# Late queries by early keys of a gated recurrence: two 128x128 products in unused PSUM columns in place of four of 64x64

## The chip, the cores and the metric

The kernel is one program on one core of a Trainium2 chip. The metric is the time of one execution on the device, in microseconds (us). Lower is better. TensorE (PE in the rows, and PEld for its weight loads), VectorE (DVE), ScalarE (ACT), GpSimd (POOL) and the DMA queue of SyncE (SP) run side by side and meet at semaphores.

## The reference, cut to what matters

The network has two layers: an HGRN2 gated linear recurrence (mixer A) and a latent attention (mixer B), for 1024 prompt positions and 8 running streams of 16 positions. Only mixer A's prompt part is touched:

```python
def gla_chunked(q, k, v, log_f, s0, chunk):       # chunk = 64, 8 heads of 128
    b = jnp.cumsum(log_f, axis=2)
    b_mid = b[:, :, mid:mid + 1]
    q_in = q * jnp.exp(b - b_mid)
    k_in = k * jnp.exp(b_mid - b)
    scores = jnp.einsum('bnlhk,bnshk->bnhls', q_in, k_in)
    scores = jnp.where(causal, scores, 0.0)
    o_intra = jnp.einsum('bnhls,bnshv->bnlhv', scores, v)
    ...
    o_inter = jnp.einsum('bnlhk,bnhkv->bnlhv', q * jnp.exp(b), s_prev)
    o = (o_intra + o_inter)
```

## The kernel before, in words

The 1024 prompt positions are 16 chunks of 64. The kernel takes them two at a time, as 8 blocks of 128. Within a block a score tile has 128 keys (partitions) by 128 queries (columns) and four quadrants of 64x64: the early chunk on itself, the late chunk on itself, late queries by early keys, and early queries by late keys, which is empty. The two diagonal quadrants come from one product of `kin` by `qin` and need a causal mask. The quadrant of late queries by early keys needs other decays, so it comes from `k_early` (the block's first 64 positions) by `q_late` (its last 64), and nothing in it is masked. Both operands hold the 8 blocks side by side, 64 columns each.

Phase A runs over 8 heads. `heads` calls `body` nine times: body h projects head h (three projections, `c` = 0, 1, 2: forget gate, query, output gate) and does the recurrence of head h-1 (`gla`) in between. A projection is 3 groups of 384 columns (`tg`) times 8 contraction tiles times 3 products of 384 columns (lines 124, 125, 126: each float32 operand is split into a high and a low part). Its three groups fill columns 0 to 383 of three PSUM banks, `pj[:, i, tg, 0:TG]`; columns 384 to 511 of these banks are not used. The other two banks, `gb`, belong to the recurrence, whose fifteen steps alternate between them.

The recurrence's TensorE work is cut into the steps of `GLA_STEPS`, put between the projection's products at fixed hooks, one hook after each 12 products. The order is written out by hand:

```python
GLA_STEPS = ["K0", "C0", "S0", "SI", "O0", "K1", "C1", "S1", "O1", "OT0", "SO", "SS0", "OT1", "SS1", "SOT"]
STEPS_AT = {3: (0, 1), 5: (2, 3), 7: (4, 5), 9: (6, 7), 11: (8, 9), 13: (10, 11), 15: (12, 13), 17: (14,)}
```

Half 0 has blocks 0 to 3, half 1 blocks 4 to 7. Of each half: K turns keys (line 510), C makes the scores (lines 539 and 544), S makes the chunk states (line 550), O makes the output from the masked scores and from the states (lines 559 and 561), OT turns the output back. Hook 3 is K0 and C0, hook 5 is S0 and SI, hook 7 is O0 and K1, hook 9 is C1 and S1, hook 11 is O1 and OT0. Hooks 3 and 9 lie behind the second of the three groups of projections 0 and 1. TensorE works strictly in this order. A step begins when what was in its bank has been read (`step_out`) and its operands are there. O1 waits for the scores of C1 (`out_of["C1"]`) and for the last state of half 1 (`state_step`).

VectorE has its own order, in `body`. Around half 1 it is: `square(0)`, `keys(1)`, the scan of the gates (line 1064), `normed(0)` (line 1002), `scores(1)` (line 964), four subtractions on the scanned gates (lines 1075 and 1077), `states(1)` (line 984, four in a chain). `scores(n)` is one predicated copy of 128x512 from PSUM to `sct`: mask 1 lets a score through, elsewhere the zeros of the start remain. In the last body (h = 8) there is no projection; the products of the output projection (128x512) stand between the steps, and `states(1)` comes directly behind `scores(1)`.

ScalarE reads a finished projection from its banks: line 773 that of `c` = 0, line 799 that of `c` = 1.

Of the kernel before, what the change touches and what calls it, by code (L numbers as in the profile page):

```python
# [13 lines left out]
P = 128  # L14
# [6 lines left out]
TG = 384  # L21
NTG = T // TG
CH = 64
# [8 lines left out]
BANK = 512  # L32
# [3 lines left out]
def flat(ap):  # L36
    return ap.rearrange("p a b -> p (a b)")
# [190 lines left out]
def phase_mixer_a(nc, k):  # L228
# [17 lines left out]
    q_late = third.take("a_q_late", [NPB, CH])  # L246
    k_early = third.take("a_k_early", [NPB, CH])
    mask_p = third.take("a_mask_p", [4 * P], I32)
# [99 lines left out]
    def buffer_of(odd, c):  # L348

        return (odd * NC + c) % 2  # L350
# [157 lines left out]
    def _(pe):  # L508
# [3 lines left out]
        def blk(x, b):  # L512
            return x[:, b * P:(b + 1) * P]

        def step(i, h):

            s = GLA_STEPS[i]
            bank = i % 2
            if i >= 2:
                step_out(pe, GLA_STEPS[i - 2], h)  # L520
            elif not (isinstance(h, int) and h == 1):

                last = len(GLA_STEPS) - 1
                pe.wait_ge(out_of[GLA_STEPS[last - (last - i) % 2]], h - 1)

            def out(slot, n=1):
                return gb[:, bank, slot * P:(slot + n) * P]

            if s in ("K0", "K1"):
                pe.wait_ge(ident_loaded, 16)  # L530
                pe.wait_ge(operand[0], h)
                for j in range(4):
                    mm = tr(bank, j, blk(kdec, 4 * int(s[1]) + j))
            elif s in ("C0", "C1"):
                pe.wait_ge(operand[1], h)
                pe.wait_ge(operand[2], h)
                for j in range(4):
                    b = 4 * int(s[1]) + j
                    nc.tensor.matmul(out(j), blk(kin, b), blk(qin, b), start=True, stop=True)  # L539
                pe.wait_ge(operand[0], h)  # L540
                pe.wait_ge(operand[3], h)
                for j in range(4):
                    b = 4 * int(s[1]) + j
                    mm = nc.tensor.matmul(gb[0:CH, bank, j * P + CH:(j + 1) * P], k_early[:, b], q_late[:, b], start=True, stop=True)
            elif s in ("S0", "S1"):
                n = int(s[1])
                pe.wait_ge(vn_loaded, h * 16)
                pe.wait_ge(out_of[f"K{n}"], h)
                for j in range(4):
                    mm = nc.tensor.matmul(out(j), kdn[:, j], vn[:, 4 * n + j], start=True, stop=True)  # L550
            elif s in ("O0", "O1"):
                n = int(s[1])
                pe.wait_ge(out_of[f"C{n}"], h)

                step_out(pe, f"S{n}", h)
                pe.wait_ge(operand[3], h)
                for j in range(4):
                    b = 4 * n + j
                    mm = nc.tensor.matmul(out(j), sct[:, j], vn[:, b], start=True, stop=b == 0)  # L559
                    if b:  # L560
                        mm = nc.tensor.matmul(out(j), blk(qex, b), st[:, b], start=False, stop=True)  # L561
            elif s in ("OT0", "OT1", "SOT"):
                n = ["OT0", "OT1", "SOT"].index(s)
                pe.wait_ge(on_ready, h * 3 + (n - 2))
                for j in range(4 if n < 2 else 1):
                    mm = tr(bank, j, on[:, j])
            elif s == "SI":
                tr(bank, 1, blk(kdec, NPB))
                mm = nc.tensor.matmul(out(2), blk(kin, NPB), blk(qin, NPB), start=True, stop=True)
            elif s == "SO":  # L570
                pe.wait_ge(out_of["SI"], h)
                pe.wait_ge(spread_done, h * 2)
                pe.wait_ge(states_loaded, h * 16)
                nc.tensor.matmul(out(0), sct8[:], vn[:, NPB], start=True, stop=False)
                for i in range(NSEQ):
                    mm = nc.tensor.matmul(out(0), qdiag[:, i], sts[:, i], start=False, stop=i == NSEQ - 1)  # L576
            else:
                n = int(s[2])
                mm = nc.tensor.matmul(out(0, 4), kd8[:], flat(vexp[:, 4 * n:4 * n + 4]), start=True, stop=True)  # L579
            mm.then_inc(pe_did[s], 1)  # L580
# [45 lines left out]
        def body(h, odd, proj, gla):  # L626
            if not proj:
                y = [k.bank[:, 4:6], k.bank[:, 0:2], k.bank[:, 2:4]]
                for i in range(-1, len(GLA_STEPS)):
                    if i >= 0:  # L630
                        step(i, h)
                    for row, t in BESIDE_STEPS.get(i, []):
                        pe.wait_ge(row_low, row + 1)
                        pe.wait_ge(o_low, parts_for(row, t))
                        if row == 0:
                            if t != 1:
                                pe.wait_ge(g_out, AH)
                            if t != 0:
                                pe.wait_ge(q_out, AH)
                        rows_product(nc, y[t], sh, row, t)  # L640
                return
            hook = 0
            for c in range(NC):
                i = buffer_of(odd, c)
                pe.wait_ge(wl_ready, h * NC + c + 1)

                if c == 2:
                    pe.wait_ge(z_out, h + 1)
                elif gla:
                    pe.wait_ge((q_out, g_out)[c], h)  # L650
                else:
                    pe.wait_ge(v_out, (len(V_UNITS) - 3, len(V_UNITS))[c])
                for tg in range(NTG):
                    for kt in range(KD):
                        cols = slice(tg * TG, (tg + 1) * TG)
                        mm = product(nc, pj[:, i, tg, 0:TG],
                                     (w_h[i][:, kt], w_l[i][:, kt]),
                                     (k.act_h[:, kt, cols], k.act_l[:, kt, cols]),
                                     kt == 0, kt == KD - 1)
                        if kt == KD - 1 and tg == NTG - 1:  # L660
                            mm.then_inc(proj_done, 1)
                        if kt % 4 == 3:
                            if gla:
                                for n in STEPS_AT.get(hook, ()):
                                    step(n, h)
                            hook += 1

        pe.wait_ge(zeroed, 1)
# [9 lines left out]
    def _(act):  # L678
# [78 lines left out]
        def body(h, odd, proj, gla):  # L757
# [9 lines left out]
            if proj:  # L767
                act.wait_ge(proj_done, h * NC + 1)
                if gla:

                    act.wait_ge(gates[2], h)
                for dst, sign in ((fz, 1.0), (nz, -1.0)):
                    last = nc.scalar.activation(dst[:].rearrange("p (a b) -> p a b", a=3), pj[:, buffer_of(odd, 0), :, 0:TG], ACT.Sigmoid, scale=sign)
                last.then_inc(z_out, 1)
                high(h, odd, 2)

                act.wait_ge(z_out, h + 1)
                if isinstance(h, int):
                    a, b = oml[:, h:h + 1], lb[:, h:h + 1]
                else:  # L780
                    a, b = oml[:, bass.ds(h, 1)], lb[:, bass.ds(h, 1)]
                if isinstance(h, int) and h == 0:
                    act.wait_ge(prep, 7)
                nc.scalar.activation(fz[:], fz[:], ACT.Ln, scale=a, bias=b).then_inc(logf_done, 1)
# [5 lines left out]
            if proj:  # L790
                act.wait_ge(proj_done, h * NC + 2)
                if gla:

                    act.wait_ge(operand[2], h)
                    act.wait_ge(operand[3], h)
                else:
                    for i in range(2):
                        act.wait_ge(v_stored[i], 16 * NT)
                nc.scalar.copy(qq[:].rearrange("p (a b) -> p a b", a=3), pj[:, buffer_of(odd, 1), :, 0:TG]).then_inc(q_out, 1)
                if not (isinstance(h, int) and h == AH - 1):  # L800
                    high(h + 1, 1 - odd, 0)
                else:
                    high_row(0)
                    high_o(0)
# [95 lines left out]
    def _(dve):  # L900
# [52 lines left out]
        def body(h, odd, proj, gla):  # L953
            def bank(s):
                return gb[:, GLA_STEPS.index(s) % 2]
# [5 lines left out]
            def scores(n):  # L961
                dve.wait_ge(zeroed, 5)
                dve.wait_ge(pe_did[f"C{n}"], h)
                nc.vector.copy_predicated(flat(sct[:]), mask_p[:], bank(f"C{n}")).then_inc(out_of[f"C{n}"], 1)

            def states(n):

# [2549 lines left out]
```

## Time and profile before

| | |
|---|---|
| median of three runs | 1863.83 us (1863.42 to 1863.83) |
| the profiled execution, whole | 1863.33 us |
| its span in the trace | 1861.5 us |
| TensorE busy | 1849.0 us, 99% of the span |
| VectorE busy | 1046.2 us, 56% |
| mean granted TensorE clock | 0.998 of full speed |

Times in the timeline are from the span's start. A row of a timeline gives the start, the time from the first start to the last end of the merged instructions, and their count. Matmuls are pipelined: the next one starts before the end of the one before, so what one costs is read from start to start. A float32 matmul of `gb` leaves two records (two passes). The recurrence of heads 1 to 7 (in bodies with a projection) lies between about 150 and 505 us, that of the last body between 505 and 550 us.

### The profile page before, as it was taken

The numbers are of one execution on the slowest core, as the hardware profiler recorded it, in microseconds if no ns is written. First come the engines' busy times: TensorE is split into PE (matmuls) and PEld (weight loads), VectorE is DVE, ScalarE is ACT, GpSimd is POOL, SyncE is SP. The second block draws the span as 40 slices with busy tenths as digits, with TensorE's granted clock in tenths as the row PEclk, the third lists the DMA queues.
The fourth block names the chain that finished last, engine by engine and source line by source line (L and its number), as shares of the span: only waits on it lengthen the run. The fifth ranks groups of instructions, "written<-read, shape, count | busy, mean of one in ns | idle before, by whom it ended". The sixth has DMA issues, their size and how long they took to land.

```text
span 1861.5 us, 30229 instructions
## 1 busy us (share of the span) xinstructions
PE 1849.0 (99%) x11250; PEld 1734.6 (93%) x11250; DVE 1046.2 (56%) x1852; ACT 741.8 (40%) x1307; POOL 429.6 (23%) x341
## 2 busy tenths in 40 slices
PE   9999999999999999999999999999999999999998
PEld 8899999999988999999999999999999999998886
DVE  3126565556768512432466676666766679853642
ACT  4234324333422221221355565555555567651100
POOL 0013133223311010000042432434324344400000
PEclk9999999999999999999999999999999999999999
DMA  8120222222255312233302111111121185553521
GB/s 264 57 87 33 76 83 84 72 83 73 70 195 164 131 46 73 83 100 120 100 27 67 42 55 55 56 51 46 51 75 38 30 255 185 189 203 127 166 86 45
DMA packets 162059, 178.91 MB, mean 96 GB/s; under 512 B 23376, under 2 KB 137424, under 8 KB 161712
## 3 DMA queue, kind: packets, MB, share of 16 engines
q1 hardware_dynamic: 155632, 158.08, 26.8%
q10 hardware_dynamic: 6160, 19.14, 2.9%
q8 instruction: 63, 1.03, 0.2%
q0 software_dynamic: 176, 0.43, 0.1%
q14 instruction: 28, 0.23, 0.0%
HBM read 130.86 MB, written 46.76 MB: 95 GB/s over the span
## 4 chain that ended last, share of the span: by engine, by line
PE 94%; DVE 2%; ACT 2%; issue 1%; DMA 1%; POOL 0%; DVEq 0%; ACTq 0%; SPq 0%; POOLq 0%
PE ps L124 27%; PE ps L126 26%; PE ps L125 26%; PE ps L2126 3%; PE ps L2105 2%; PE ps L2104 2%; PE ps L550 1%; PE ps L510 1%; PE ps L576 1%; PE ps L559 1%; PE ps L579 1%; ACT h_p L2239 1%; PE ps L539 1%; PE ps L561 1%; PE ps L2682 1%
## 5 line engine op out<-in xcount | busy, mean ns | idle before, releaser
L2016 POOL TENSOR_SCALAR h_p<-h_p,h_rsum 128x128 f32<-128x128 f32 (+3 forms) x127 | 217.8, 1717 | 420.5 <-DVE h_rsum L2368 420.1
L124 PE MATMUL ps<-act_h,a_w_l 128*128 128x384 f32 x576 | 202.0, 351 | 0.0
L126 PE MATMUL ps<-act_h,a_w_h 128*128 128x384 f32 x576 | 192.9, 335 | 0.0
L125 PE MATMUL ps<-act_l,a_w_h 128*128 128x384 f32 x576 | 192.8, 335 | 0.0
L124 PE MATMUL ps<-act_h,m_c_l 128*128 128x384 f32 x480 | 160.9, 335 | 0.0
L126 PE MATMUL ps<-act_h,m_c_h 128*128 128x384 f32 x480 | 160.4, 334 | 0.0
L125 PE MATMUL ps<-act_l,m_c_h 128*128 128x384 f32 x480 | 160.4, 334 | 0.0
L118 DVE TENSOR_TENSOR h_pt_l<-ps,h_pt_h 128x128 fp32r<-128x128 f32 (+2 forms) x192 | 100.5, 552 | 60.2 <-ACT h_pt_h L113 59.8
L113 ACT ACTIVATE h_pt_h<-ps 128x128 fp32r<-128x128 f32 (+2 forms) x192 | 86.8, 489 | 88.3 <-PE ps L2126 88.1
L2239 ACT ACTIVATE h_p<-ps,h_mx 128x128 f32<-128x128 f32 (+7 forms) x128 | 94.8, 741 | 67.1 <-DVE h_mx L2364 66.7
L124 PE MATMUL ps<-o_w,o_g 128*128 128x512 f32 x288 | 112.3, 390 | 0.0
L126 PE MATMUL ps<-o_w,o_g 128*128 128x512 f32 x288 | 112.1, 389 | 0.0
L125 PE MATMUL ps<-o_w,o_g 128*128 128x512 f32 x288 | 112.1, 389 | 0.0
L124 PEld LDWEIGHTS ps<-act_h,a_w_l 128*128 128x128 f32 x576 | 108.2, 188 | 4.1 <-issue 3.3
L125 PEld LDWEIGHTS ps<-act_l,a_w_h 128*128 128x128 f32 x576 | 108.3, 188 | 3.4 <-issue 3.4
L126 PEld LDWEIGHTS ps<-act_h,a_w_h 128*128 128x128 f32 x576 | 108.1, 188 | 0.0
L124 PE MATMUL ps<-cq_h,h_w_l 128*128 128x384 f32 x288 | 102.1, 354 | 0.6
L2364 DVE TENSOR_REDUCE h_mx<-ps 128x1 f32<-128x128 f32 (+7 forms) x128 | 97.0, 758 | 4.4
L126 PE MATMUL ps<-cq_h,h_w_h 128*128 128x384 f32 x288 | 96.8, 336 | 0.0
L125 PE MATMUL ps<-cq_l,h_w_h 128*128 128x384 f32 x288 | 96.7, 336 | 0.0
L124 PEld LDWEIGHTS ps<-act_h,m_c_l 128*128 128x128 f32 x480 | 90.1, 188 | 0.0
L125 PEld LDWEIGHTS ps<-act_l,m_c_h 128*128 128x128 f32 x480 | 90.1, 188 | 0.0
(326 smaller groups left out, 4955.0 us busy)
## 6 DMA issues: line engine op xcount, KB each, us to landing
a_w_raw<-in_w_in_a SPq DMA_DIRECT2D x24, 512.0 KB, 5.0
m_c_raw<-in_w_in_b SPq DMA_DIRECT2D x20, 512.0 KB, 4.2
scratch_gate<-m_sg SPq DMA_DIRECT2D x16, 576.0 KB, 5.2
o_w_raw<-in_w_out_b SPq DMA_DIRECT2D x16, 512.0 KB, 5.8
h_gate<-scratch_gate SPq DMA_DIRECT2D x60, 128.0 KB, 2.0
scratch_og<-h_gate SPq DMA_DIRECT2D x60, 128.0 KB, 1.7
s_ct_raw<-in_cache_ckv_turned SPq DMA_DIRECT2D x7, 1024.0 KB, 5.2
o_g_raw<-scratch_og SPq DMA_DIRECT2D x24, 256.0 KB, 4.5
```

The costliest lines, as they stand in the source:

```text
L113: return nc.scalar.activation(high, x, ACT.Identity)
L118: return nc.vector.tensor_tensor(low, x, high.bitcast(F32), ALU.subtract)
L124: nc.tensor.matmul(out, ll, rh, start=first, stop=False)
L125: nc.tensor.matmul(out, lh, rl, start=False, stop=False)
L126: return nc.tensor.matmul(out, lh, rh, start=False, stop=last)
L510: return nc.tensor.transpose(gb[:, bank, slot * P:(slot + 1) * P], src, k.ident[:])
L2016: nc.gpsimd.tensor_scalar(x, x, rsum[:, u % PB], None, ALU.mult).then_inc(S["p_ready"], 1)
L2104: nc.tensor.matmul(out, rq[:, e, q], k.kr_l[:, kc], start=False, stop=False)
L2105: mm = nc.tensor.matmul(out, rq[:, e, q], k.kr_h[:, kc], start=False, stop=True)
L2126: mm = nc.tensor.transpose(bank[:, 4 + i % TB, j * P:j * P + P], p[:, u % PB, key * P:(key + 1) * P], k.ident[:])
L2239: nc.scalar.activation(weights_of(u), scores_of(u), ACT.Exp, bias=mx[:, u % PB], accum_out=rsum[:, u % PB]).then_inc(S["exp_done"], 1)
L2364: nc.vector.tensor_reduce(mx[:, u % PB], scores_of(u), AX.X if n <= BANK else AX.XY, ALU.max, negate=True).then_inc(S["max_done"], 1)
```

## The change

In bodies that have a projection, the products of late queries by early keys are made two blocks at a time: `k_early` of two neighbouring blocks is the 128-column stationary operand, `q_late` of the same two blocks the 128-column moving one. Of the 128x128 result only the two 64x64 quadrants on the diagonal are wanted; the other two cross the blocks and are not read. The two products of a step go to columns 384 to 511 of the first two banks of the projection that is running, whose groups are closed by then. Four products of 64x64 in the step's own bank fall away. In the last body they stay as they were.

On VectorE `scores` becomes four instructions (three in the last body): a predicated copy of the upper left quadrants (64 partitions, 4x64 columns), one of the lower right quadrants, and plain copies of the late-by-early quadrants: two of 64 partitions by 2x64 from the projection's banks, the second of which reads partitions 64 to 127 and writes 0 to 63; or, in the last body, one of 4x64. ScalarE waits for C0's and C1's copies before it reads the projection's banks, because its release lets later products into them.

```diff
-        def step(i, h):
+        def step(i, h, late=None):
...
-                for j in range(4):
-                    b = 4 * int(s[1]) + j
-                    mm = nc.tensor.matmul(gb[0:CH, bank, j * P + CH:(j + 1) * P], k_early[:, b], q_late[:, b], start=True, stop=True)
+                if late is None:
+                    for j in range(4):
+                        b = 4 * int(s[1]) + j
+                        mm = nc.tensor.matmul(gb[0:CH, bank, j * P + CH:(j + 1) * P], k_early[:, b], q_late[:, b], start=True, stop=True)
+                else:
+                    for j in range(2):
+                        two = slice(4 * int(s[1]) + 2 * j, 4 * int(s[1]) + 2 * j + 2)
+                        mm = nc.tensor.matmul(late[:, j, TG:BANK], flat(k_early[:, two]), flat(q_late[:, two]), start=True, stop=True)
...
-                                    step(n, h)
+                                    step(n, h, pj[:, i])
...
                 if gla:
-
+                    act.wait_ge(out_of["C0"], h)
                     act.wait_ge(gates[2], h)
...
                 if gla:
-
+                    act.wait_ge(out_of["C1"], h)
                     act.wait_ge(operand[2], h)
...
-                nc.vector.copy_predicated(flat(sct[:]), mask_p[:], bank(f"C{n}")).then_inc(out_of[f"C{n}"], 1)
+                at = bank(f"C{n}").rearrange("p (a b) -> p a b", a=4)
+                mask = mask_p[:].rearrange("p (a b) -> p a b", a=4)
+                for rows, cols in ((slice(0, CH), slice(0, CH)), (slice(CH, P), slice(CH, P))):
+                    last = nc.vector.copy_predicated(sct[rows, :, cols], mask[rows, :, cols], at[rows, :, cols])
+                if proj:
+                    wide = pj[:, buffer_of(odd, n), 0:2, TG:BANK]
+                    for half in range(2):
+                        rows = slice(half * CH, half * CH + CH)
+                        last = nc.vector.tensor_copy(sct[0:CH, half:4:2, CH:P], wide[rows, :, rows])
+                else:
+                    last = nc.vector.tensor_copy(sct[0:CH, :, CH:P], at[0:CH, :, CH:P])
+                last.then_inc(out_of[f"C{n}"], 1)
```

## Rows read from the trace of the kernel before

**Rows 1.** The page: busy time of the engines, granted clock, the chain's shares.
```profile
PE 1849.0 (99%) x11250; PEld 1734.6 (93%) x11250; DVE 1046.2 (56%) x1852; ACT 741.8 (40%) x1307; POOL 429.6 (23%) x341
...
PE 94%; DVE 2%; ACT 2%; issue 1%; DMA 1%; POOL 0%; DVEq 0%; ACTq 0%; SPq 0%; POOLq 0%
```

**Rows 2.** Waits of PE over the whole span: total, times, longest (us).
```profile
PE ps L550 <- DVE a_kdn L959: 0.3, 1, 0.3
...
PE ps L539 <- DVE a_qin L1128: 0.2, 1, 0.2
```

**Rows 3.** Timeline of PE at hook 5 of one head: start, length (us), instructions.
```profile
313.05 0.33 PE L126 MATMUL ps<-act_h,a_w_h 128*128 128x384 f32 x1
313.22 1.05 PE L550 MATMUL ps<-a_vn,a_kdn 128*128 128x128 f32 x8
314.11 0.27 PE L510 MATMUL ps<-ident,a_kdec 128*128 128x128 f32 x1
314.22 0.39 PE L569 MATMUL ps<-a_qin,a_kin 128*128 128x128 f32 x2
...
314.62 0.33 PE L125 MATMUL ps<-act_l,a_w_h 128*128 128x384 f32 x1
```

**Rows 4.** Timeline of PE at hook 3 of the same head.
```profile
306.90 0.60 PE L510 MATMUL ps<-ident,a_kdec 128*128 128x128 f32 x4
307.33 1.06 PE L539 MATMUL ps<-a_qin,a_kin 128*128 128x128 f32 x8
308.32 0.68 PE L544 MATMUL ps<-a_q_late,a_k_early 128*64 128x64 f32 x8
308.93 0.44 PE L124 MATMUL ps<-act_h,a_w_l 128*128 128x384 f32 x1
309.21 0.34 PE L125 MATMUL ps<-act_l,a_w_h 128*128 128x384 f32 x1
```

**Rows 5.** Timeline of PE at hook 9 of the same head.
```profile
324.79 1.05 PE L539 MATMUL ps<-a_qin,a_kin 128*128 128x128 f32 x8
325.77 0.68 PE L544 MATMUL ps<-a_q_late,a_k_early 128*64 128x64 f32 x8
326.38 1.16 PE L550 MATMUL ps<-a_vn,a_kdn 128*128 128x128 f32 x8
...
327.55 0.34 PE L125 MATMUL ps<-act_l,a_w_h 128*128 128x384 f32 x1
```

**Rows 6.** Timeline of PE at hook 11 of the same head.
```profile
331.59 0.46 PE L559 MATMUL ps<-a_vn,a_sct 128*128 128x128 f32 x2
331.89 0.39 PE L561 MATMUL ps<-a_st,a_qex 128*128 128x128 f32 x2
332.11 0.39 PE L559 MATMUL ps<-a_vn,a_sct 128*128 128x128 f32 x2
```

**Rows 7.** Timeline of PEld at hook 11 of the same head.
```profile
331.56 0.30 PEld L559 LDWEIGHTS ps<-a_vn,a_sct 128*128 128x128 f32 x2 [0.15 <-issue]
```

**Rows 8.** Groups by shape, 130 to 550 us: busy, mean ns, idle before.
```profile
L559 PEld LDWEIGHTS ps<-a_vn,a_sct 128*128 128x128 f32 x128 | 19.2, 191 | 1.3 <-issue 1.1
...
L964 DVE COPY_PREDICATED a_sct<-a_mask_p,ps 128x512 f32<-128x512 int32 x16 | 11.8, 740 | 8.4 <-PE ps L544 8.2
...
L959 DVE COPY a_kdn<-ps 128x512 f32<-128x512 f32 x16 | 11.0, 686 | 28.3 <-PE ps L510 28.3
...
L1045 DVE COPY_PREDICATED a_sct<-a_mask_s,ps 128x128 f32<-128x128 int32 x8 | 2.4, 295 | 0.0
```

**Rows 9.** Timeline of DVE around C1 and O1 of the same head.
```profile
326.56 0.73 DVE L964 COPY_PREDICATED a_sct<-a_mask_p,ps 128x512 f32<-128x512 int32 x1 [0.32 <-PE ps L544]
327.18 1.41 DVE L1075 TENSOR_TENSOR a_bm<-a_bb 128x1024 f32<-128x1024 f32 x2
328.51 1.42 DVE L1077 TENSOR_TENSOR a_nz<-a_bb 128x1024 f32<-128x1024 f32 x2
329.85 1.49 DVE L984 SCALAR_TENSOR_TENSOR a_st<-a_st,a_decay_b,ps 128x128 f32<-128x128 f32 x4
```

**Rows 10.** Timeline of DVE at C0 and after it, same head.
```profile
309.11 0.76 DVE L964 COPY_PREDICATED a_sct<-a_mask_p,ps 128x512 f32<-128x512 int32 x1 [0.81 <-PE ps L544]
314.31 0.29 DVE L980 COPY a_st<-ps 128x128 f32<-128x128 f32 x1 [4.45 <-PE ps L550]
...
315.67 0.28 DVE L1044 COPY a_kd<-ps 128x128 f32<-128x128 f32 x1
315.87 0.29 DVE L1045 COPY_PREDICATED a_sct<-a_mask_s,ps 128x128 f32<-128x128 int32 x1
```

**Rows 11.** Timeline of DVE in the attention phase, rope sums (line 2326).
```profile
922.14 1.12 DVE L2326 TENSOR_TENSOR h_p<-h_p 64x384 f32<-64x384 f32 x2
```

**Rows 12.** Timeline of ACT at the end of projection 0, same head.
```profile
313.42 1.13 ACT L773 ACTIVATE a_fz<-ps 128x1152 f32<-128x1152 f32 x1 [11.25 <-PE ps L126]
```

**Rows 13.** Timeline of DVE in the last body, around O1.
```profile
524.61 0.74 DVE L964 COPY_PREDICATED a_sct<-a_mask_p,ps 128x512 f32<-128x512 int32 x1
525.24 1.48 DVE L984 SCALAR_TENSOR_TENSOR a_st<-a_st,a_decay_b,ps 128x128 f32<-128x128 f32 x4
```

**Rows 14.** Timeline of PE in the last body, at O1.
```profile
527.28 0.39 PE L561 MATMUL ps<-a_st,a_qex 128*128 128x128 f32 x2
```

## The prediction, made before the changed kernel ran

> **What bounds the kernel now.** I read the page first: TensorE is busy 99% of the span and is 94% of the chain that ended last, VectorE is busy 56% [rows 1]. So a change counts by what it takes from TensorE's own work and by what it makes TensorE wait for. The chain of waits shows almost no wait of TensorE in this phase: one of 0.3 us and one of 0.2 us [rows 2]. That view names only idle time of the engine, and a pipelined matmul that starts late hides in a longer record; so I went on to the timelines, start to start, of the hooks that the change touches.
>
> A plain float32 pass of 128x128: at hook 5 the records of S0 and SI, 8 + 1 + 2 = 11, run from 313.22; the second projection product behind them starts at 314.62, and a steady product takes 0.17 (313.05 to 313.22), so they cost 314.45 - 313.22 = 1.23 us, or 0.111 each [rows 3]. Hook 3 costs 309.21 - 0.17 - 306.90 = 2.14 us; take away its 4 + 8 = 12 records of 0.111 (1.33) and the eight records of line 544 cost 0.81 us [rows 4]. Hook 9 gives the same: 327.55 - 0.17 - 324.79 = 2.59, less 16 x 0.111 = 1.78, leaves 0.81 [rows 5]. Of it 0.61 us lies between line 544's first start and the next instruction's; 0.10 lies ahead (line 539's eight records should take 0.89 and take 0.99 at 307.33), and 0.10 behind. The trace marks these records as a tile of 128 by 64 where all others are 128 by 128.
>
> The second place is O1. Its first record starts at 331.59, but line 561 behind it only at 331.89, 0.30 later instead of 0.22 (as from 331.89 to 332.11) [rows 6], and its weight load started 0.15 us late [rows 7]; over the heads this is 1.1 us of idle weight loading on line 559 [rows 8], some 0.15 for each of seven. What it waited for is `states(1)`, whose last instruction ends at 329.85 + 1.49 = 331.34 [rows 9]. VectorE is thus already the bound from C1 to O1: scores at 326.56, four subtractions, four states, nothing idle between.
>
> **The change part by part.** *Removed on TensorE:* eight records of line 544, 0.81 us a step. *Added:* 2 products x 2 passes x 0.111 = 0.445 us. Gain 0.36 us a step, in 14 steps (7 heads x 2), 5.1 us if nothing else moved. Whether the two gaps of 0.10 go too has to be chosen. In favour: hook 3's passage from line 510 to line 539 also has waits in it, but takes 0.43 for four records, no gap [rows 4]; only the narrow records have gaps, on both sides, and behind them no wait stands. I take both as gone. The bound is that both stay: then the gain is 0.17 us a step. The Trainium skill, TensorEngine Tiling (Array Packing), Key Properties, says that changing the tiling mode drains the engine; by it, both gaps go, as in my sum. No row can separate the two causes ahead of line 544.
>
> *Added on VectorE:* one predicated copy of 512 columns becomes two of 256 and two plain copies of 128. By the columns: predicated 0.740 at 512 and 0.295 at 128, so 0.44 at 256 [rows 8]; plain copies 0.28 [rows 10]. Start to start, usually a row is less than its length: line 964 takes 0.73 but the next starts 0.62 later [rows 9], line 1044 takes 0.28, the next starts 0.20 later [rows 10]. That overlap need not hold here, since the partitions change. The nearest row is line 2326: two sums of 64x384, the first reading the lower, the second the upper 64 partitions; together they take 1.12 [rows 11], two lengths of 0.55 end to end with 0.01 between. So changed start partitions cost the overlap. I take it for all four passages, to the second, third and fourth instruction and to what follows (whose inputs start at 0 again, after the mask read from 64): 2 x (0.44 + 0.01) + 2 x (0.28 + 0.01) = 1.49, against 0.62 before: +0.87 us. Lower bound, all overlaps kept: 2 x 0.34 + 2 x 0.20 = 1.08, +0.45 us. Upper, if a copy that shifts partitions needs twice its columns' time: another 2 x 0.13 us; line 2326 speaks against that, since it shifts too and costs what its columns say.
>
> For these four passages the Trainium skill, VectorE: DVE Perf Modes, "Two Vector instructions with no wait between them", has a rule: an instruction whose first input from a memory, or whose output, starts in another group of 32 partitions than the last one did is held until all before it are finished. It speaks against this change. By it all four are held, +0.87 us; by the usual overlap alone it would be +0.45. Rows 11 agree with it for one kind of passage; the passage back from the mask's upper half no row shows.
>
> *Where the longer scores lie.* At C0 (half 0) VectorE then idles 4.45 us until S0 [rows 10], so +0.87 is covered; ScalarE's new wait is satisfied at about 309.11 - 0.16 + 1.5 = 310.5, and it reads the projection only from 313.42 [rows 12]. At C1 ScalarE reads even later against it. At C1 the longer scores lie on the path to O1. Step by step, from C1's first start (324.79): the late products' last pass ends 0.16 us earlier (its start at 0.89 + 3 x 0.111 = 1.22, length 0.27 as line 510's last record [rows 3]; before, the end was 325.77 + 0.68 = 326.45, that is at 1.66). VectorE was idle 0.32 us ahead of the scores, so it starts 0.16 earlier [rows 9]. Then +0.87: `states(1)` ends 0.71 us later, at 332.05 in the old times. From its end to line 561 it was 331.89 - 331.34 = 0.55 [rows 6, 9]; so line 561 starts at 332.60, 0.71 later than before. TensorE itself would have been ready earlier, so all of hook 9's gain becomes waiting. Per head: -0.36 at hook 3, +0.71 at hook 11 = +0.35; seven heads: +2.4 us. Behind O1 the engines are in step again: VectorE next waits for OT0, as before. The stall sits between O1's waits and everything behind O1 in TensorE's queue, and nothing gives it back.
>
> *The last body:* no product changes. `scores` is 2 x 0.45 + one copy of 256 (0.42 by 0.686 at 512 and 0.28 at 128, + 0.01) = 1.34, against 0.63 [rows 13]: +0.70. `states(1)` follows directly and ends at 526.72 [rows 13]; line 561 starts at 527.28, 0.56 behind it [rows 14], the same distance as in the waiting heads, so there is no slack: +0.7 us. At its C0, VectorE had 0.3 us idle and O0 comes later; hidden.
>
> **Sum:** +2.4 + 0.7 = +3.1 us on the profiled execution: span 1861.5 to 1864.6, its time 1863.33 to 1866.4. The median of the runs lies 0.5 above that execution: 1863.83 + 3.1 = 1867.0 us (+0.17%).
>
> **Rivals.**
>
> *No passage on VectorE is held.* Then scores cost +0.45 (last body: 2 x 0.34 + 0.33 - 0.63 = +0.38). Per head -0.36 + 0.45 - 0.16 = -0.07, times 7 = -0.5, and +0.4: 1863.7 us. Line 2326 speaks against it.
>
> *Slower: the two gaps of 0.10 stay on TensorE* (they come from the waits, or from float32 columns beside the split products). Hook 3 then gains 0.17; C1 ends only 0.06 earlier, so O1 comes 0.81 later: +0.64 a head, 4.5 + 0.7 = +5.2: 1869.0 us. It decides against "no change" as soon as a head loses 0.43 us instead of 0.35, because 0.2% is 3.7 us: a margin of 0.08 us. A shifted copy at double time has the same result (8 x 0.27 = +2.1 more).
>
> *Faster: O1 doesn't wait,* because scores(1) turns out to be covered. Then 14 x 0.36 = 5.1 us and the present stall (7 x 0.08) go: 1858.2 us. Against it: no idle time of VectorE between scores and states [rows 9], and the late weight load in seven heads [rows 7, 8].
>
> **How the numbers follow.** Changes within 0.2% (3.7 us) of the median can't be told from none. Chances: forecast 0.56 (0.48 of it inside 0.2%, 0.08 above), nothing held 0.12, gaps stay or dearer copies 0.25, O1 doesn't wait 0.05, something else slower 0.02. Faster 0.05, same 0.60, slower 0.35. The range takes in the unheld case and the gaps that stay: 1863.4 to 1869.4. The forecast's own range is 1866.0 to 1868.0.
>
> **What would show it.** Hook 3's span falls from 2.14 to 1.78 us. The four instructions of scores start 0.45, 0.45, 0.29 and 0.29 apart. `states(1)` ends about 7.26 after C1's start (6.55 before) and line 561 of O1 starts at 7.81 (7.10 before), while PE shows idle time at line 559 of 0.5 us or more a head. The last body's O1 comes 0.7 later behind its C1. I would be wrong if scores(1) starts later than the end of C1 demands, if the copies have other lengths than their columns, or if a wait of TensorE shows up at another hook.

## The result, and the profile after

The changed kernel takes 1868.31 us (median of 10 runs, 1867.63 to 1869.4), the kernel before 1863.35 us (median of 10 runs): ratio 1.0028, 95% interval 1.002 to 1.0036. It is slower by 5.0 us. The prediction had 1867.0 us with a range of 1863.4 to 1869.4, which holds the time; but it took a change within 0.2% for likelier (0.60) than a slower kernel (0.35), and the measured median lies just beyond 0.2%, with the lower end of the interval at 0.2%. The prediction added 3.1 us to an earlier median of the kernel before (1863.83), so its 1867.0 is 1.3 us short, but its change is 1.9 us short of the 5.0 measured.

The profiled execution has a span of 1866.2 us, 4.7 us more than before. Its page: TensorE is busy 4 us less, VectorE 16 us more, and in the chain that ended last VectorE's share went from 2% [rows 1] to 4%.

```profile
span 1866.2 us, 30170 instructions
PE 1845.0 (99%) x11194; PEld 1732.1 (93%) x11194; DVE 1061.9 (57%) x1898; ACT 742.8 (40%) x1307; POOL 430.1 (23%) x341
...
PE 92%; DVE 4%; issue 2%; ACT 2%; DMA 1%; POOL 0%; DVEq 0%; ACTq 0%; SPq 0%; POOLq 0%
```

The waits of PE over the whole span now name what was hidden before: O1 (line 564 here) waits for `states(1)` (line 1000) in all eight heads, and a step of the last body waits for the scores of C0 (line 979).

```profile
PE ps L564 <- DVE a_st L1000: 8.5, 8, 1.1
...
PE ps L510 <- DVE a_sct L979: 0.4, 1, 0.4
```

The same head on PE: hook 3, which answers to [rows 4], then hooks 9 and 11, which answer to [rows 5, 6].

```profile
308.63 0.60 PE L510 MATMUL ps<-ident,a_kdec 128*128 128x128 f32 x4
309.07 1.06 PE L539 MATMUL ps<-a_qin,a_kin 128*128 128x128 f32 x8
309.96 0.61 PE L549 MATMUL ps<-a_q_late,a_k_early 128*128 128x128 f32 x4
310.32 0.42 PE L124 MATMUL ps<-act_h,a_w_l 128*128 128x384 f32 x1
310.58 0.34 PE L125 MATMUL ps<-act_l,a_w_h 128*128 128x384 f32 x1
...
326.17 1.05 PE L539 MATMUL ps<-a_qin,a_kin 128*128 128x128 f32 x8
327.06 0.61 PE L549 MATMUL ps<-a_q_late,a_k_early 128*128 128x128 f32 x4
...
328.57 0.34 PE L125 MATMUL ps<-act_l,a_w_h 128*128 128x384 f32 x1
...
333.86 0.46 PE L564 MATMUL ps<-a_vn,a_sct 128*128 128x128 f32 x2 [1.14 <-DVE a_st L1000]
334.16 0.39 PE L566 MATMUL ps<-a_st,a_qex 128*128 128x128 f32 x2
```

Hook 3 costs 310.58 - 0.17 - 308.63 = 1.78 us, as forecast (2.14 before); hook 9 costs 328.57 - 0.17 - 326.17 = 2.23 (2.59 before). TensorE's own gain is there in full, 0.36 us a step. But line 566 starts 334.16 - 326.17 = 7.99 us behind C1's start, against 331.89 - 324.79 = 7.10 before. DVE of the same head, the answer to [rows 9]:

```profile
327.77 0.90 DVE L972 COPY_PREDICATED a_sct<-a_mask_p,ps 64x256 f32<-64x256 int32 x2 [0.16 <-PE ps L549]
328.69 0.59 DVE L977 COPY a_sct<-ps 64x128 f32<-64x128 f32 x2
329.31 1.43 DVE L1091 TENSOR_TENSOR a_bm<-a_bb 128x1024 f32<-128x1024 f32 x2
330.65 1.42 DVE L1093 TENSOR_TENSOR a_nz<-a_bb 128x1024 f32<-128x1024 f32 x2
332.11 1.50 DVE L1000 SCALAR_TENSOR_TENSOR a_st<-a_st,a_decay_b,ps 128x128 f32<-128x128 f32 x4
```

The scores start 1.60 us behind C1's start (1.77 before) and take 329.31 - 327.77 = 1.54 us to the start of the subtractions, against 0.62. From there to the first state it is 2.80 us, against 329.85 - 327.18 = 2.67: the last subtraction ends at 330.65 + 1.42 = 332.07 and the first state starts behind that, where before it started 0.08 ahead of its predecessor's end (328.51 + 1.42 = 329.93 against 329.85).

Per head that is -0.36 (hook 3) + 0.89 = +0.53 us, and from one head's C0 to the next head's it is 52.65 us on the mean against 52.12; seven heads make 3.7 of the 4.7 us. The last body gives 0.8 (from its C0 to line 566 17.40 us against 16.61). The remaining 0.2 us lies ahead of the first head's C0 (151.14 us from the span's start against 150.98), where nothing was changed; behind the last O1 the two traces are equally long (1334.25 us).

### The profile page after: what moved, and what is told of

Read it like the earlier page. It is cut to its first block, busy times and chain, and to the rows that moved or that the text cites. A ratio compares the mean times of both kernels' runs of the same rounds, so it can differ in the third digit from the quotient of the medians.

```text
span 1866.2 us, 30170 instructions
## 1 busy us (share of the span) xinstructions
PE 1845.0 (99%) x11194; PEld 1732.1 (93%) x11194; DVE 1061.9 (57%) x1898; ACT 742.8 (40%) x1307; POOL 430.1 (23%) x341
## 4 chain that ended last, share of the span: by engine, by line
PE 92%; DVE 4%; issue 2%; ACT 2%; DMA 1%; POOL 0%; DVEq 0%; ACTq 0%; SPq 0%; POOLq 0%
PE ps L124 26%; PE ps L125 26%; PE ps L126 26%; PE ps L2142 3%; PE ps L2121 2%; PE ps L2120 2%; PE ps L564 1%; PE ps L510 1%; PE ps L581 1%; PE ps L584 1%; ACT h_p L2255 1%; PE ps L539 1%; PE ps L2698 1%; PE ps L566 1%; DVE a_st L1000 1%
```

## Experiments

The runs were made in three groups, each with its own runs of the kernel before. The time that a run is compared with is the median of those (1863.56, 1863.48 and 1863.50 us).

### The two halves of the change, alone

`pe_alone`, the changed kernel with the old scores:

```diff
-                for rows, cols in ((slice(0, CH), slice(0, CH)), (slice(CH, P), slice(CH, P))):
...
-                last.then_inc(out_of[f"C{n}"], 1)
+                nc.vector.copy_predicated(flat(sct[:]), mask_p[:], bank(f"C{n}")).then_inc(out_of[f"C{n}"], 1)
```

> This kernel leaves out the use of the late products: scores is the one predicated copy of 128x512 of before, from the step's own bank, in which nothing is computed for late queries by early keys. So the change on TensorE stands alone. Theory (the longer scores on VectorE are the whole loss): hook 3 costs 1.78 us as in the changed kernel, C1 ends 0.16 us earlier, states(1) too, and O1's line 566 starts 0.16 us earlier behind C1's start; per head -0.36 - 0.16 = -0.52 us, seven heads -3.6, the last body unchanged: 1863.35 - 3.6 = 1859.7 us. Rival (part of the loss comes from products in the projection's banks, or from ScalarE's two new waits): above 1863 us, with a stall of O1 longer than in the kernel before.

Measured: 1860.66 us against 1863.56, ratio 0.9985 (0.9976 to 0.9994); span 1858.2. The timeline of PE in one head, C1's first products and O1:

```profile
322.89 0.94 PE L539 MATMUL ps<-a_qin,a_kin 128*128 128x128 f32 x7
...
329.54 0.46 PE L564 MATMUL ps<-a_vn,a_sct 128*128 128x128 f32 x2
329.83 0.39 PE L566 MATMUL ps<-a_st,a_qex 128*128 128x128 f32 x2
```

Line 566 starts 6.94 us behind C1's start, 0.16 earlier than before, to the hundredth what the theory says, and 0.52 us a head are gained. The median gains 2.9 us instead of 3.6, the span 3.3; the last body is 0.3 us longer in this execution (its source is below, under Left open). ScalarE's new waits and the products in the projection's banks are in this kernel, and cost nothing in these heads.

`dve_alone`, TensorE as before and four instructions in scores:

```diff
-                nc.vector.copy_predicated(flat(sct[:]), mask_p[:], bank(f"C{n}")).then_inc(out_of[f"C{n}"], 1)
...
+                for rows, cols in ((slice(0, CH), slice(0, CH)), (slice(CH, P), slice(CH, P))):
+                    last = nc.vector.copy_predicated(sct[rows, :, cols], mask[rows, :, cols], at[rows, :, cols])
+                if proj:
+                    for half in range(2):
+                        rows = slice(half * CH, half * CH + CH)
+                        last = nc.vector.tensor_copy(sct[0:CH, half:4:2, CH:P], at[rows, half:4:2, CH:P])
...
```

> TensorE does the four 64x64 products of before; scores has the four instructions of the changed kernel. The last of them reads scores of the partitions 64 to 127 of the step's own bank, so late-by-early scores of every second block are other numbers. Theory: C0's longer scores are covered, C1's are not: scores cost +0.91 us, the first instruction of states(1) another 0.1 because it is held, so O1 comes 1.0 us later a head, seven heads +7.1, the last body +0.85: 1871.3 us. Rival (the loss comes from TensorE's side or ScalarE's waits): within 1 us of 1863.35.

Measured: 1871.56 us, ratio 1.0043 (1.0029 to 1.0056). PE in one head:

```profile
328.61 0.83 PE L539 MATMUL ps<-a_qin,a_kin 128*128 128x128 f32 x6
...
336.75 0.39 PE L561 MATMUL ps<-a_st,a_qex 128*128 128x128 f32 x2
```

8.14 us from C1's start to line 561, +1.04 a head. So the whole loss is VectorE's, and in the seven heads it is as large as the sum says: 1.04 x 7 = 7.3. That the rest fits too is partly luck: in the profiled execution (span +8.3) the last body gives only 0.4 us instead of 0.85, and 0.7 us lie ahead of the first head's C0 (151.69 against 150.98), where nothing was changed.

### Taking the longer scores off the path

`after_states_first` moves `states(1)` ahead of the four subtractions, which O1 does not need; `before_states_first` does the same to the kernel before.

```diff
                     normed(0)
                     scores(1)
+                    states(1)
                 dve.wait_ge(b_step, h * 2 + 1)
...
                 if gla:
-                    states(1)
                     if isinstance(h, int) and h == AH - 1:
```

> The changed kernel, with states(1) put directly behind scores(1), ahead of the four subtractions. Theory: states(1) then ends at about 4.7 us behind C1's start, and TensorE gets to O1 only at 6.4, so O1 doesn't wait: per head -0.36 at hook 3, -0.36 at hook 9 and the stall of before, -0.10, gone; seven heads -5.8, last body +0.85, rest of the phase +0.2: 1858.6 us, provided ScalarE's exponentials, which need the subtractions, still find them done. Rival (they become the new wait, 1.5 us later than before): O1 quick, but a wait of TensorE at hook 3 or 13, and not under 1863 us.

> The kernel before with the same reordering alone. Theory: only the stall of 0.10 us a head at O1 goes: 1863.35 - 0.7 = 1862.6 us. Rival (the reordering is worth something by itself): 1861 us or less.

Measured: 1859.51 us against 1863.56, ratio 0.9978 (0.9969 to 0.9987), and 1863.03 us, ratio 0.9998 (0.9989 to 1.0007). The first kernel's head on DVE:

```profile
323.85 0.90 DVE L972 COPY_PREDICATED a_sct<-a_mask_p,ps 64x256 f32<-64x256 int32 x2 [0.16 <-PE ps L549]
324.76 0.59 DVE L977 COPY a_sct<-ps 64x128 f32<-64x128 f32 x2
325.39 1.50 DVE L1000 SCALAR_TENSOR_TENSOR a_st<-a_st,a_decay_b,ps 128x128 f32<-128x128 f32 x4
326.80 1.42 DVE L1092 TENSOR_TENSOR a_bm<-a_bb 128x1024 f32<-128x1024 f32 x2
328.14 1.42 DVE L1094 TENSOR_TENSOR a_nz<-a_bb 128x1024 f32<-128x1024 f32 x2
```

and on PE:

```profile
322.24 0.83 PE L539 MATMUL ps<-a_qin,a_kin 128*128 128x128 f32 x6
...
328.63 0.38 PE L564 MATMUL ps<-a_vn,a_sct 128*128 128x128 f32 x2
328.86 0.39 PE L566 MATMUL ps<-a_st,a_qex 128*128 128x128 f32 x2
```

The states end at 326.89, 1.7 us ahead of O1, and O1 no longer waits: line 566 starts 6.62 behind C1's start. The subtractions end at 329.56; the exponential that needs them starts only at 332.70 on ScalarE (in the kernel before they end at 329.93 and it starts at 335.63), both times behind work that follows TensorE. The same scores, held passages and all (a passage leads from one VectorE instruction to the next, and is held when the next starts only behind the end of the one before), now cost nothing in these heads: a head takes 51.30 us instead of 52.12. In the last body, where `states(1)` stood directly behind `scores(1)` all along, O1 still waits 0.5 us. The profiled execution (1858.69 us) is close to the 1858.6 expected; why the median lies 0.9 us above that is not known. In the kernel before the reordering can take only the 0.10 us a head that O1 waited there (line 561 at 7.00 instead of 7.10, which its trace shows); 0.7 us is less than this comparison can tell from none.

### What makes the four instructions dear

`same_start` keeps their number and sizes but lets all start at partition 0:

```diff
-                nc.vector.copy_predicated(flat(sct[:]), mask_p[:], bank(f"C{n}")).then_inc(out_of[f"C{n}"], 1)
...
+                low, early, late = slice(0, CH), slice(0, CH), slice(CH, P)
+                nc.vector.copy_predicated(sct[low, :, early], mask[low, :, early], at[low, :, early])
+                nc.vector.copy_predicated(spare[low], mask[low, :, late], at[low, :, late])
...
+                        last = nc.vector.tensor_copy(sct[low, half:4:2, late], at[low, half:4:2, late])
...
```

> TensorE as before; scores has two predicated copies of 64x256 and two plain ones of 64x128, like the changed kernel, but all of them start at partition 0, reading and writing. It leaves out the lower right quadrants (the second predicated copy goes to a spare tile). Theory (the passages between start partitions cost the overlap): the four start 0.34, 0.34, 0.20 and 0.20 us apart, states(1) ends 7.00 us behind C1's start, line 566's counterpart 7.55, seven heads +3.2, last body +0.5: 1867.2 us. Rival (four short instructions cost this wherever they start): as dve_alone, 7.59 and 1871.5 us.

Measured: 1866.86 us, ratio 1.0019 (1.001 to 1.0028). DVE of one head:

```profile
327.85 0.43 DVE L968 COPY_PREDICATED a_sct<-a_mask_p,ps 64x256 f32<-64x256 int32 x1 [0.32 <-PE ps L545]
328.19 0.43 DVE L969 COPY_PREDICATED a_spare<-a_mask_p,ps 64x256 f32<-64x256 int32 x1
328.52 0.47 DVE L972 COPY a_sct<-ps 64x128 f32<-64x128 f32 x2
328.92 1.41 DVE L1086 TENSOR_TENSOR a_bm<-a_bb 128x1024 f32<-128x1024 f32 x2
```

The starts are 0.34, 0.33, 0.20 and 0.20 us apart, as expected. That is 1.07 us from the first start to the subtractions, where the changed kernel has 1.54 (dve_alone, with the same work on TensorE as here, 1.53) and the kernel before 0.62. So of the extra 0.92 us some 0.45 are the larger number of instructions and columns, and 0.47 the four lost overlaps.

`copies_swapped` exchanges the two copies from the projection's banks:

```diff
-                    for half in range(2):
+                    for half in (1, 0):
                         rows = slice(half * CH, half * CH + CH)
```

> The changed kernel, with the two copies from the projection's banks in the other order: the one that reads partitions 64 to 127 first. Theory (an instruction is held when it reads PSUM from another start partition than the last reader of PSUM): the number of held passages within scores stays, but the first instruction of states(1), which reads PSUM from partition 0, now follows a reader from 0 and starts ahead of its predecessor's end as in the kernel before; states(1) ends 7.32 us behind C1's start instead of 7.44, seven heads -0.8: 1867.5 us. Rival (its late start comes from something else): 7.44 and 1868.3 us.

DVE of one head:

```profile
328.80 0.59 DVE L977 COPY a_sct<-ps 64x128 f32<-64x128 f32 x2
329.42 1.43 DVE L1091 TENSOR_TENSOR a_bm<-a_bb 128x1024 f32<-128x1024 f32 x2
330.77 1.42 DVE L1093 TENSOR_TENSOR a_nz<-a_bb 128x1024 f32<-128x1024 f32 x2
332.10 1.49 DVE L1000 SCALAR_TENSOR_TENSOR a_st<-a_st,a_decay_b,ps 128x128 f32<-128x128 f32 x4
```

The first state starts at 332.10, before its predecessor's end at 332.19 again, and line 566 7.87 behind C1's start (334.15 - 326.28) instead of 7.99. The mechanism is shown by the trace, in each of the seven heads: a copy four instructions earlier had left its mark. The time did not show it: 1868.3 us, ratio 1.0025 (1.0015 to 1.0035), where 1867.5 was expected; 0.8 us is less than such a comparison can tell from none. In its profiled execution, whose span is 0.7 us longer than the changed kernel's, the seven heads are 0.8 us shorter. Against that stand 0.5 us ahead of the first head's C0 (151.61 against 151.14) and 1.1 us in the last body. There VectorE's `scores(1)` stand behind the low part of the second weight row of the output projection, which came later. The row on ScalarE and the scores on VectorE, first of the changed kernel, whose C0 in this body starts at 514.52:

```profile
522.87 1.06 ACT L113 ACTIVATE m_w_h<-m_w_raw 128x1024 fp32r<-128x1024 f32 x1 [1.78 <-DMA m_w_raw<-in_w_out_a]
...
528.52 0.90 DVE L972 COPY_PREDICATED a_sct<-a_mask_p,ps 64x256 f32<-64x256 int32 x2
```

and of copies_swapped, with C0 at 514.20:

```profile
523.60 1.06 ACT L113 ACTIVATE m_w_h<-m_w_raw 128x1024 fp32r<-128x1024 f32 x1 [3.27 <-DMA m_w_raw<-in_w_out_a]
...
529.25 0.89 DVE L972 COPY_PREDICATED a_sct<-a_mask_p,ps 64x256 f32<-64x256 int32 x2
```

The scores start 5.65 us behind the row in both. The row comes 8.35 us behind C0 in the first and 9.40 in the second.

### What the narrow products cost on TensorE

`waits_ahead` is the kernel before with the two waits ahead of line 544's products moved ahead of line 539's. `four_of_128x64` is the changed kernel with four late products of 64 moving columns by the 128 stationary columns of two blocks.

```diff
                 pe.wait_ge(operand[2], h)
+                pe.wait_ge(operand[0], h)
+                pe.wait_ge(operand[3], h)
...
-                pe.wait_ge(operand[0], h)
-                pe.wait_ge(operand[3], h)
```

```diff
-                    for j in range(2):
...
+                    for j in range(4):
+                        b = 4 * int(s[1]) + j
+                        two = slice(b - j % 2, b - j % 2 + 2)
+                        at = TG + (j % 2) * CH
+                        mm = nc.tensor.matmul(late[:, j // 2, at:at + CH], flat(k_early[:, two]), q_late[:, b], start=True, stop=True)
```

> The kernel before, with the two waits that stand between the products of line 539 and the 64x64 ones moved ahead of the former. Theory (change of tile): hook 3 stays 2.14 us, line 544's counterpart starts 0.99 us behind C0's start, 1863.5 us. Rival (the waits make the gap ahead of the narrow products): it starts 0.89 behind, hook 3 2.04, per head -0.2, -1.4: 1862.1 us.

> The changed kernel, but the late products are four of 64 moving columns by the 128 stationary columns of two blocks, in the projection's free columns: as many and as short matmuls as before, in the full tile. Theory (the two gaps of 0.10 us come from the change of tile): no gaps. If a pass is bound by its moving columns, hook 3 costs 1.33 + 8 x 0.057 = 1.79 us and the time is that of the changed kernel, 1868.3; if by its 128 weight columns, 8 x 0.111: 2.22 us, hook 3 costs 0.44 more; C1 ends later too, 0.44 x 14 = +6.2: 1874.5 us. Rival (short matmuls cause the gaps): 1.99 to 2.14 us at hook 3.

Measured: 1863.34 us (ratio 1.0, 0.9991 to 1.0009) and 1873.59 us (1.0055, 1.0041 to 1.0069). Hook 3 on PE, first with the waits ahead:

```profile
307.36 1.06 PE L541 MATMUL ps<-a_qin,a_kin 128*128 128x128 f32 x8
308.35 0.68 PE L544 MATMUL ps<-a_q_late,a_k_early 128*64 128x64 f32 x8
```

and with four products in the full tile:

```profile
311.67 1.06 PE L539 MATMUL ps<-a_qin,a_kin 128*128 128x128 f32 x8
312.57 1.00 PE L551 MATMUL ps<-a_q_late,a_k_early 128*128 128x64 f32 x8
...
313.64 0.34 PE L125 MATMUL ps<-act_l,a_w_h 128*128 128x384 f32 x1
```

The gap ahead of the narrow products stays (0.99 us for line 541's eight records) with no wait between; in the full tile it is gone (0.90), though the matmuls are as many and have as few moving columns. So neither the waits nor the few moving columns make the gaps; they come with the tile of 128 by 64, as the prediction chose. A tile of 128 by 64 and a stationary operand of 64 columns go together in all these kernels, so no run tells the change of tile from the narrower operand. The eight records of 64 moving columns cost 313.64 - 0.17 - 312.57 = 0.90 us or 0.112 each, as much as with 128 moving columns. In the 64x64 products steady starts are 0.058 us apart (three from 308.43 to 308.60 in the kernel before), so of line 544's 0.81 us only 8 x 0.058 = 0.46 are passes. The other 0.35, an estimate by this difference, go with the narrow tile; the prediction's two gaps of 0.10 are only a part of it.

### The version that beats both

`states_first_last_body_old`: `states(1)` first, and in the last body the one predicated copy of before.

```diff
+                if not proj:
+                    nc.vector.copy_predicated(flat(sct[:]), mask_p[:], bank(f"C{n}")).then_inc(out_of[f"C{n}"], 1)
+                    return
...
```

> The changed kernel with states(1) directly behind scores(1), and in the last body the one predicated copy of before. Theory: the seven heads are those of after_states_first, -5.8 us against the kernel before, and the last body gives back its 0.85: 1858.7 us. Rival (the last body's loss has another source): 1859.5 us, as after_states_first.

Measured: 1858.82 us against 1863.50, ratio 0.9975 (0.9965 to 0.9985). The heads are as in after_states_first. The median is 0.7 us lower, as the theory has it, but the trace of the last body does not show the gain: from C0 to line 566 it takes 17.55 us, against 17.44 in after_states_first and 16.61 before. The scores take 0.73 us less, but the weight row came 9.23 us behind C0 instead of 8.37, VectorE's keys(1) stand behind it, and TensorE waits 1.0 us for them, against 0.3 before [rows 2]. So the 0.7 us between the medians of two groups is not shown to come from the last body's scores.

```profile
PE ps L555 <- DVE a_kdn L964: 1.0, 1, 1.0
```

## Why the prediction was right or wrong, point by point

**TensorE's gain, both gaps gone:** right, 0.36 us a step, shown in the trace after; waits_ahead and four_of_128x64 rule out the waits and the few moving columns as the cause of the gaps.

**The longer scores and where they lie:** right in mechanism. The start 0.16 us earlier (0.17 measured, and by the prediction's own 1.66 - 1.49), the covered C0 in the seven heads and the path C1, scores, states, O1 came out as written; pe_alone and dve_alone divide the two sides, and after_states_first shows the place. The term "+0.87 us" (2 x 0.45 + 2 x 0.29 is 1.48, not 1.49, so +0.86) was 0.92: the passage to the subtractions leaves a pause of 0.03 us, not 0.01, and the lengths are a few hundredths longer.

**`states(1)` ends 0.71 us later:** this is the step that failed, in size. It took every VectorE instruction behind the scores at its old spacing. The first state reads PSUM from partition 0, the last of the new copies had read PSUM from partition 64, and the four instructions between read none; so the state was held too, +0.12 us. With the 0.05 above, O1 came 0.89 us later instead of 0.71: +0.53 a head, not +0.35, and +3.7, not +2.4. copies_swapped took the 0.12 us away by changing nothing but the order of two copies. The prediction's margin, 0.08 us a head to the threshold of 0.2%, was smaller than this, and so "same" got most of the chance and "slower" came. The time lies above the forecast's own range (1866.0 to 1868.0). The wide range holds it only because it takes in the rivals at 1869.0 (gaps that stay, a dearer shifted copy), and neither happened: that it holds is luck.

**The last body, +0.7 us, all of it at O1, C0 hidden:** the sum was right (0.79 us), and so was the path: from the start of `scores(1)` to line 566 it is 3.40 us against 527.28 - 524.61 = 2.67 [rows 13, 14]. A wait of TensorE was missed, which the prediction itself had named as a sign of being wrong. The first state of half 0 was indeed late by little, but the step SI turns keys in the bank of C0 and waits for that bank's scores: TensorE waited 0.4 us there (line 979 in the waits), and C1 starts 0.33 us later. This adds nothing to the sum, because `scores(1)` does not wait for C1 there: it starts 5.65 us behind the second weight row's start on ScalarE, in the changed kernel (522.87 and 528.52) as in the kernel before, whose scores start at 524.61 [rows 13]:

```profile
518.96 1.06 ACT L113 ACTIVATE m_w_h<-m_w_raw 128x1024 fp32r<-128x1024 f32 x1 [1.83 <-DMA m_w_raw<-in_w_out_a]
```

So O1 comes only 0.46 us later behind C1, and not the 0.7 that was named as the sign.

**The rivals:** nothing held is ruled out by same_start (0.47 us cheaper than what was measured); staying gaps by the trace after; the faster one, with O1 not waiting, did not happen by itself, but it is what after_states_first makes: 6.62 us to line 566. No copy cost twice its columns: the shifted one takes 0.59 us together with the unshifted one. (That rival was priced in eight bodies, but the last one has no shifted copy; 7 x 0.27 is 1.9 us, not 2.1.)

**Left open:** what sets the arrival of the second weight row in the last body. It starts on ScalarE between 7.91 (dve_alone) and 9.40 us (copies_swapped) behind C0, and the scores start 5.65 us behind it in the trace of every kernel here, so the last body varies by up to 1.5 us with something that no run controlled. The stretch ahead of the first head's C0 varies by 0.7 us as well (150.98 before, 151.69 in dve_alone). Both blur medians where a kernel differs by less.

## What to carry to other kernels

An engine that is busy half of the time can be the bound in one stretch: look for the instruction that starts late inside a longer record, and count the work between its releaser and the last common point. When work is moved from the busy engine to another one, first move the dependent result ahead of what nobody waits for yet; here this turned a loss of 5.0 us into a gain of 4.1, with the same instructions (4.7 with the old copy in the last body). And here splitting one VectorE instruction by partitions cost more than its columns, also in a later instruction that wasn't touched.

## What the runs showed of the hardware

The hold outlasts other instructions. With a last reader of PSUM at partition 64, the first state, with four instructions between, started 0.03 us behind its predecessor's end instead of 0.08 ahead; with the last reader at partition 0 (copies_swapped) it started 0.08 ahead again. The Trainium skill, VectorE: DVE Perf Modes, "Two Vector instructions with no wait between them", states just this, since it keeps the start of the last reader for each memory apart; the traces agree (0.12 us), and I had applied it only to the passages inside the scores.

A float32 pass with 128 stationary columns cost 0.112 us with 64 moving columns and 0.111 with 128; with 64 by 64 it cost half, 0.058. At these sizes the stationary columns set the time. The Trainium skill, TensorE: Matmul & The Clock Gate, "LDWEIGHTS (loading the stationary operand)", gives for the load of the stationary operand its columns divided by 1.2 in ns, so 107 and 53 by this estimate. The spacing of the passes agrees to some 5 ns; the records of the loads are longer, 191 ns on the mean for 128 columns [rows 8].
